# A two-block transformer kernel: attention sums that leave their result as columns, and transposes that also divide

## The reference, cut to what matters

```
# first block, each layer: six heads that share one k and one v
logits = q·k * 64 ** -0.5, -inf where the index or the causal mask says so
p = softmax(logits);  a_out = p @ v
mix = concatenate([a_out, b_out, c_out]) @ w_out[l];  x = x + g1 * mix

# second block, layer 0 (forgetting attention), 16 heads, each with its own v
s = q·k * scale + c_q - c_k;  o = softmax(s, causal) @ v;  h = h + o @ w_out

# second block, layer 1 (sparse attention), 16 heads, v shared by 8 heads
e_c = exp(s_c - max(s_c)) * m_c;  p_c = e_c / max(sum(e_c), 1.0)     # 15 compressed keys
o = g[0] * (p_c @ vc) + g[1] * (softmax(s_s) @ vs) + g[2] * (softmax(s_w) @ vw)
h = h + o @ w_out
```

## Time and profile before

| | |
|---|---|
| median of 3 runs | 2928.42 us (2925.82 to 2932.46) |
| the profiled execution | 2925.72 us, of it 2923.8 us span |
| PE busy | 2451.6 us, 84% of the span |
| DVE busy | 1976.5 us, 68% |
| ACT busy | 1412.9 us, 48% |
| attention of the first block, layer 0 | 178.4 to 198.3 us |
| the same, layer 1 | about 705 to 725 us |
| forgetting attention | 2081.7 to 2144.6 us |
| sparse attention | 2551.3 to 2687.6 us |

### The profile page before, as it was taken

The page is one execution under the profiler, slowest core; times in us unless marked ns, Lnnn a source line. Parts: engine busy times, 40 slices in busy tenths (PEclk is TensorE's granted clock), DMA queues, the critical chain, the costliest instruction groups (busy, mean ns, idle before and its releaser), DMA issues.

```text
span 2923.8 us, 31822 instructions
## 1 busy us (share of the span) xinstructions
PE 2451.6 (84%) x13007; PEld 2110.9 (72%) x13007; DVE 1976.5 (68%) x2434; ACT 1412.9 (48%) x1353; POOL 28.0 (1%) x52
## 2 busy tenths in 40 slices
PE   5847799883585999999999999959479975588898
PEld 4736699763464888888888888847479965567898
DVE  6555654756564888888888888865448864444787
ACT  5322444432332777777777777753334432344432
POOL 0000000000000000000000000000000000000000
PEclk9957899986686999999999999989689985666999
DMA  8501755741052999999999999974025541200453
GB/s 328 162 1 33 244 188 187 271 140 49 4 173 96 376 337 356 357 355 357 347 347 355 355 358 356 356 226 145 29 67 187 188 147 38 94 1 25 148 185 113
DMA packets 293723, 590.78 MB, mean 202 GB/s; under 512 B 11702, under 2 KB 86564, under 8 KB 292928
## 3 DMA queue, kind: packets, MB, share of 16 engines
q1 hardware_dynamic: 289872, 572.33, 55.5%
q0 software_dynamic: 3696, 16.32, 1.8%
HBM read 587.56 MB, written 1.05 MB: 201 GB/s over the span
## 4 chain that ended last, share of the span: by engine, by line
PE 60%; DVE 5%; ACT 2%; DMA 1%; issue 1%; POOL 0%; DVEq 0%; SPq 0%; ACTq 0%
PE ps L1084 17%; PE ps L1086 17%; PE ps L1085 17%; PE ps L1184 2%; PE ps L1167 1%; PE ps L1152 1%; PE ps L1282 1%; DVE arena L1589 1%; PE ps L1265 1%; PE ps L1243 1%; PE ps L1121 1%; PE ps L1138 1%; DVE arena L1732 0%; DVE Z L1598 0%; DVE Z L1589 0%
## 5 line engine op out<-in xcount | busy, mean ns | idle before, releaser
L764 ACT ACTIVATE w_hi<-raw 128x2048 fp32r<-128x2048 f32 x548 | 1041.9, 1906 | 635.1 <-PE ps L1086 505.0
L1574 DVE TENSOR_TENSOR w_lo<-raw,w_hi 128x2048 fp32r<-128x2048 f32 x548 | 1225.2, 2273 | 54.1 <-ACT w_hi L764 38.0
L1084 PE MATMUL ps<-w_hi,xT_hi 128*128 128x512 f32 (+3 forms) x1600 | 637.3, 398 | 43.0 <-DVE xT_lo L1678 24.3
L1086 PE MATMUL ps<-w_hi,xT_lo 128*128 128x512 f32 (+3 forms) x1600 | 623.4, 390 | 0.0
L1085 PE MATMUL ps<-w_lo,xT_hi 128*128 128x512 f32 (+3 forms) x1600 | 622.9, 389 | 0.0
L1084 PEld LDWEIGHTS ps<-w_hi,xT_hi 128*128 128x128 f32 x1600 | 306.5, 192 | 109.8 <-DVE xT_lo L1678 25.7
L1085 PEld LDWEIGHTS ps<-w_lo,xT_hi 128*128 128x128 f32 x1600 | 306.9, 192 | 62.3 <-issue 3.3
L1086 PEld LDWEIGHTS ps<-w_hi,xT_lo 128*128 128x128 f32 x1600 | 305.6, 191 | 62.2
L1084 PE MATMUL ps<-xT_hi,w_hi 128*128 128x256 f32 (+1 forms) x1120 | 324.6, 290 | 15.2 <-DVE xT_lo L2270 11.0
L1085 PE MATMUL ps<-xT_lo,w_hi 128*128 128x256 f32 (+1 forms) x1120 | 324.3, 290 | 0.0
L1086 PE MATMUL ps<-xT_hi,w_lo 128*128 128x256 f32 (+1 forms) x1120 | 324.1, 289 | 0.0
(11 more groups left out here) (315 smaller groups left out, 2052.8 us busy)
## 6 DMA issues: line engine op xcount, KB each, us to landing
raw<-in_moe_w_gate SPq DMA_DIRECT2D x112, 1024.0 KB, 5.4
raw<-in_moe_w_up SPq DMA_DIRECT2D x112, 1024.0 KB, 5.4
raw<-in_moe_w_down SPq DMA_DIRECT2D x112, 1024.0 KB, 5.5
raw<-in_w_ada SPq DMA_DIRECT2D x48, 1024.0 KB, 5.3
raw<-in_f_w_up SPq DMA_DIRECT2D x44, 1024.0 KB, 5.0
raw<-in_f_w_down SPq DMA_DIRECT2D x22, 1024.0 KB, 5.0
raw<-in_w_in SPq DMA_DIRECT2D x20, 1024.0 KB, 6.3
raw<-in_a_w_in SPq DMA_DIRECT2D x12, 1024.0 KB, 5.1
```

The costliest lines, as they stand in the source:

```text
L764: act.activation(w_hi[:, k % HI, 0:LEN[k]], raw[:, r, 0:LEN[k]], ACT.Copy).then_inc(w_hi_ready, 1)
L1084: pe.matmul(out_, lh, rh, start=start, stop=False)
L1086: return pe.matmul(out_, ll, rh, start=False, stop=stop)
L1574: dve.tensor_tensor(w_lo[:, k % RAW, 0:LEN[k]], raw[:, k % RAW, 0:LEN[k]], w_hi[:, k % HI, 0:LEN[k]].bitcast(F32), ALU.subtract).then_inc( ...
```

## The change

Three things change together, in all four attentions.

**The sums are turned.** The values become the stationary operand (64 columns) and the transposed probabilities the moving one. The result has features on the partitions: heads of even number on partitions 0 to 63, of odd number on 64 to 127, 128 tokens wide. Where heads share their values (first block, sparse attention) two heads of one parity go in one product of 256 columns. That is the column layout of the next linear: `out_high` (ScalarE) and `out_low` (VectorE) split the bank straight into `xT_hi` and `xT_lo`. The three parts of the sparse attention are now added in the bank by TensorE (`first`, `last`), one evacuation for three parts.

**The division moves.** Since tokens are now along the free dimension, the inverse row sum can't be multiplied on afterwards. `scaled(i)` on VectorE computes the inverses, multiplies with the gate, and writes a 128x512 tile of four diagonal matrices; the transposes of the probabilities become matmuls whose moving operand is that diagonal instead of the identity. They wait for `att_scaled`.

**`to_columns` goes.** Before `fa_out` and `nsa_out` it is removed; before `out0` and `out1` it starts at chunk 3 (ten tiles instead of sixteen).

```diff
@@ TensorE, transposed(i)
-                    if kind == "few":
-                        pe.wait_ge(att_probs, at.few(i))
-                    else:
-                        pe.wait_ge(att_exp, at.scored(i))
...
-                            last = pe.transpose(ps[0:kw, 6 + u // 4, (u % 4) * P:(u % 4 + 1) * P],
-                                                bufs[at.nth[i] % 3][:, x:x + kw], ident)
+                    pe.wait_ge(att_scaled, at.scored(i))
...
+                             last = pe.matmul(ps[0:kw, 6 + u // 4, (u % 4) * P:(u % 4 + 1) * P],
+                                              bufs[at.nth[i] % 3][:, x:x + kw],
+                                              diags[at.nth[i] % 2][:, h * P:(h + 1) * P], start=True, stop=True)
@@ TensorE, sums(i)
-                    for h in range(nh):
-                        for c in range(nch):
-                            u = h * nch + c
-                            last = pe.matmul(ps[:, 2 + s % 2, h * HD:(h + 1) * HD], Ts[s % 2][0:kw, u * P:(u + 1) * P],
-                                             v(h, c), start=c == 0, stop=c == nch - 1)
+                    n_v, shared = nh // 2, len(v) == 1
+                    for parity in range(2):
+                        out_ = ps[HD * parity:HD * parity + HD, 2 + o % 2, :]
+                        for j in range(1 if shared else n_v):
+                            w = n_v * P if shared else P
+                            for c in range(nch):
+                                x = ((c * 2 + parity) * n_v + j) * P
+                                last = pe.matmul(out_[:, j * P:j * P + w], v[0 if shared else 2 * j + parity](c),
+                                                 Ts[s % 2][0:kw, x:x + w], start=at.first[i] and c == 0,
+                                                 stop=at.last[i] and c == nch - 1)
@@ VectorE, in place of kept(i) and taken(i)
+                def scaled(i):
...
+                    dve.wait_ge(att_exp, at.scored(i))
+                    if kind == "few":
+                        x = bufs[s % 3][:, 0:nh * 256].rearrange("p (h w) -> p h w", h=nh)[:, :, 0:W]
+                        tt(x, x, kept.unsqueeze(1).to_broadcast([P, nh, W]), ALU.mult)
+                        step(dve.tensor_reduce(total, x, AX.X, ALU.add))
                     ts(total, total, 1.0, ALU.max)
                     step(dve.reciprocal(inverse, total))
+                    if weight is not None:
+                        tt(inverse, inverse, weight, ALU.mult)
...
+                    dve.tensor_tensor(diags[s % 2][:, 0:nh * P].rearrange("p (h t) -> p h t", h=nh),
+                                      ident.unsqueeze(1).to_broadcast([P, nh, P]),
+                                      inverse.unsqueeze(2).to_broadcast([P, nh, P]), ALU.mult).then_inc(att_scaled, 1)
...
+                for k in range(n + 4):
                     if k < n and at.parts[k][0] != "heads":
                         maxima(k)
-                    if 0 <= k - 3 < n and at.parts[k - 3][0] != "heads":
-                        taken(k - 3)
-                    if 0 <= k - 1 < n and at.parts[k - 1][0] == "few":
-                        kept(k - 1)
+                    if 0 <= k - 1 < n and at.parts[k - 1][0] != "heads":
+                        scaled(k - 1)
+                    if k >= 4 and at.last[k - 4]:
+                        out_low(k - 4)
@@ ScalarE, VectorE: the split into columns
+                    act.activation(hi, ps[:, 2 + o % 2, 0:at.parts[i][1] * HD].rearrange("p (k t) -> p k t", t=P),
+                                   ACT.Copy).then_inc(att_high, 1)
...
+                    dve.wait_ge(att_high, at.outs(i))
+                    dve.tensor_tensor(lo, ps[:, 2 + o % 2, 0:at.parts[i][1] * HD].rearrange("p (k t) -> p k t", t=P),
+                                      hi.bitcast(F32), ALU.subtract).then_inc(att_taken, 1)
@@ before the output linears
-                to_columns(mix)
+                to_columns(mix, 3)
                 linear(f"out{l}")
...
-            to_columns(mix)
             linear("fa_out")
...
-            to_columns(mix)
             linear("nsa_out")
```

More of the change, by code:

```diff
@@ L117, in __init__ @@
     def __init__(self, parts, count):
-        self.parts, self.nth, self._at = parts, [], []
+        self.parts, self.nth, self.first, self.last, self._at = [], [], [], [], []
         n = 0
-        for kind, _, _ in parts:
+        for kind, nh, W, turn in parts:
+            self.parts.append((kind, nh, W))
             self.nth.append(n)
+            self.first.append(turn in ("first", "only"))
+            self.last.append(turn in ("last", "only"))
             n += kind != "heads"
@@ L124, in __init__ @@
             count["scored"] += kind != "heads"
-            count["few"] += kind == "few"
+            count["outs"] += self.last[-1]
             self._at.append(dict(count))
@@ L132, in scored, with outs @@
         return self._at[i]["scored"]
-    def few(self, i):
-        return self._at[i]["few"]
+    def outs(self, i):
+        return self._at[i]["outs"]
     def scored_part(self, s):
@@ L490, in build @@
         att_T, fa_T, nsa_T = (attT, attT_b), (attT2, attT2b), (attT2, attT2c)
-        count = {"all": 0, "scored": 0, "few": 0}
-        dsa = [Attention([("full", nh, (b + 1) * P) for b in range(TB) for nh in (4, 2)], count) for _ in range(2)]
-        both = [("heads", 4, 66)] * 2
-        four = [("full", 4, (b + 1) * P) for b in range(TB)]
+        att_diag, late_diag = (diag_a, diag_b), (mix[:, 0, 0:512], mix[:, 0, 512:1024])
+        count = {"all": 0, "scored": 0, "outs": 0}
+        dsa = [Attention([("full", nh, (b + 1) * P, "only") for b in range(TB) for nh in (4, 2)], count) for _ in range(2)]
+        both = [("heads", 4, 66, None)] * 2
+        four = [("full", 4, (b + 1) * P, "only") for b in range(TB)]
         fa = Attention(both + both + four + both + four + both + four + four, count)
-        one = [("heads", 2, P)]
+        one = [("heads", 2, P, None)]
         def of_head(x, h):
@@ L503, in twice, with columns_of, dsa_places @@
             return x.unsqueeze(2).to_broadcast(shape)
-        six = [(kind, 4, W) for b in range(TB) for kind, W in (("few", N_CMP), ("full", (b + 1) * P), ("full", (b + 1) * P))]
+        six = [(kind, 4, W, turn) for b in range(TB) for kind, W, turn in
+               (("few", N_CMP, "first"), ("full", (b + 1) * P, None), ("full", (b + 1) * P, "last"))]
         nsa = Attention(one + one + six + one + six + one + six + six, count)
+        def columns_of(first, pairs, b):
+            return [x[:, first:first + pairs, b * P:(b + 1) * P] for x in (xT_hi, xT_lo)]
+        def dsa_places(i):
+            return columns_of(2 * (i % 2), 2 - i % 2, i // 2)
+        fa_places, nsa_places = (lambda i, at=at: columns_of(2 * ((at.outs(i) - at.outs(0) - 1) // TB), 2,
+                                                             (at.outs(i) - at.outs(0) - 1) % TB) for at in (fa, nsa))
         ar.at = a1
@@ L828, in experts, with to_columns @@
                 expert_rows(k)
-            def to_columns():
-                for k in range(4):
+            def to_columns(first=0):
+                for k in range(first // 2, 4):
+                    c = max(first, 2 * k)
                     act.wait_ge(tr_psum, got(tr_psum))
-                    act.activation(xT_hi[:, 2 * k:2 * k + 2, :],
-                                             ps[:, k, :].rearrange("p (k t) -> p k t", k=2), ACT.Copy).then_inc(xT_hi_ready, 1)
+                    act.activation(xT_hi[:, c:2 * k + 2, :],
+                                   ps[:, k, :].rearrange("p (k t) -> p k t", k=2)[:, c - 2 * k:2, :],
+                                   ACT.Copy).then_inc(xT_hi_ready, 1)
             def square_sums(src):
@@ L980, in _ @@
                 root(stat_b[:, 0:2])
-                to_columns()
+                to_columns(3)
                 linear(f"out{l}")
@@ L1113, in linear, with to_columns @@
                 got(lin_evac, min(2, gi))
-            def to_columns(src):
+            def to_columns(src, first=0):
                 pe.wait_ge(rows_ready, got(rows_ready))
-                for k in range(4):
-                    for c in (2 * k, 2 * k + 1):
+                for k in range(first // 2, 4):
+                    for c in range(max(first, 2 * k), 2 * k + 2):
                         for b in range(TB):
@@ L1739, in maxima @@
                                       ALU.mult).then_inc(att_centred, 1)
[L1741 to L1752 removed]
+                def scaled(i):
+                    kind, nh, W = at.parts[i]
+                    _, weight, kept = ops[i]
                     s = at.nth[i]
```

134 lines of the change are left out of this document (54 added, 80 removed).

## The result

The changed kernel takes 2955.05 us (median of 4 runs, 2951.05 to 2955.66), the kernel before 2930.44 in the runs beside it (4 runs, 2925.82 to 2933.10): a ratio of 1.0083, 95% interval 1.0070 to 1.0096. It is slower by 24.6 us; 17 were forecast. The profiled executions span 2952.9 and 2923.8 us, 29.1 apart: that of the kernel before took 2925.72 us, 4.7 under its median, that of the changed kernel 2954.88, its median, so the traces show a few us more than the medians do.

What follows compares the result with a forecast made beforehand. PE was taken as the bound, with gaps. Sparse attention +13 and -4.2, forgetting attention +8 and -5.1, first block +5.2 make +17 us on the median 2928.4: forecast 2945 us, range 2918 to 2980.

Steps and rivals of the forecast that it cites:

- The ring: In the attentions: scores, maxima of a part, diagonals and transposes of the part before, next scores; takes over 15.9 us of waits.
- part 2: Diagonals: `scaled` takes 1.35 us, 0.5 more on few parts; a sparse-attention group 39.9 us at half clock, 28.9 at full.
- rival (d): Diagonal products run in one pass; a sparse-attention group takes 33 or 25.5 us, about -13 in all, 2915 us; chance 5%.
- I take 45% of the time at full: PE's clock in the sparse attention: 45% of the time at full, so a group takes 34.1 us, the stage 149.
- rival (a): Wide products keep PE's clock at full; sparse attention 126 us, -28 in all, 2900 us; chance 15%, mostly 2900 to 2925.
- rival (b): PE's clock stays where it is or falls; all at half: sparse attention 174 us, +72, 3000; 15% for 2962 and more.
- The forgetting attention: Later first transposes and doubled passes over four groups, +8 us; its tail goes, -5.1 us.
- the second ones can start 0.6 to 0.9 us later: Forgetting attention: second transposes of a pair start 0.6 to 0.9 us later and take 16 passes instead of 8.
- The first block: Per layer 18 transposes become 36 passes and `scaled` is in the chain, +4 us; `to_columns` -1.4; two layers +5.2.
- The turned product costs what the old one did.: Turned sums, four heads, 128 keys at half clock: 1.76 us before, 1.71 after; one pass saved per part, 0.4 us.
- rival (c): Halves of the sums overlap fully: nothing in the sparse attention, -8 us in the forgetting one, 2937 us; chance 10%.
- PE the bound, with gaps: Kernel before, attention stages: PE busy 114.9 of 136.3 us in the sparse attention, 48.7 of 62.9 in the forgetting one.

Runs made afterwards that it cites:

- wait, one pass: Changed kernel with the diagonal step computed and waited for, but transposes by the identity in one pass, diagonals unused and division left out: 2927.05 us.
- experiment 2: Changed kernel with the sums of odd heads sent to the same 64 output partitions as even heads and added there: 2950.14 us.
- scores first: TensorE issues scores of part k ahead of the transposes of part k-2: changed kernel 2878.80 us, kernel before 2879.81 us.
- experiment 6: Kernel before, with the transposes of exponentials made matrix products by the identity, two passes instead of one: 2923.19 us, ratio 0.9973.
- experiment 1: Three kernels from the changed one: no diagonal step, one-pass transposes, 2869.01 us; the same, two passes, 2870.74; diagonals waited for but unused, one pass, 2927.05.

## Why the prediction was right, and where it wasn't

**The direction and the mechanism were right.** The ring that part 2 of the prediction set up is the one that the timeline shows, and it is what the transposes wait for: 43.4 us in 21 waits in the sparse attention. Both ways of cutting it (TensorE's order, VectorE's order) take time off, 76 and 40 us, of the 76 some 26 more than the same order takes off the kernel before. The diagonal tile takes 0.69 us as the earlier trace rows said (686 ns). Two passes per diagonal product, which rival (d) doubted, are there, at 0.23 us each at half clock (16 in 3.68) where 0.214 was taken. Of the signs that the prediction named, the sparse attention's clock (0.65, near 0.72 expected), its length (158, 145 to 155) and the forgetting attention's (74, near 71) were missed. All three stages were dearer than forecast.

**The ring's prices were right; the clock in it was not.** The prediction gave a group of the sparse attention 39.9 us at half clock and 28.9 at full, with 13 us around four groups. A granted clock of 0.65 means 30% of the time at full (0.5 + 0.5 x 0.30). Then a group takes 1 / (0.70 / 39.9 + 0.30 / 28.9) = 35.8 us, and the stage 4 x 35.8 + 13 = 156 us; 158.1 was measured. The same sum with the clock of other kernels that keep this ring:

| kernel | clock | the prediction's sum at that clock | measured |
|---|---|---|---|
| changed | 0.65 | 156 | 158.1 |
| sums on one half | 0.76 | 146 | 145.2 |
| products in the wait | 0.96 | 131 | 131.6 |
| wait, one pass (33 and 25.5 a group, from rival (d)) | 0.58 | 139 | 136.1 |

The step that failed is "I take 45% of the time at full": it was 30%. It makes 7 of the 9 us by which the sparse attention was mis-sized (158.1 against 149). The 45% were leaned on the forgetting attention's 0.74. Why the clock here stayed under it the runs don't show. The prediction named the ring's idle time under rival (a), as what speaks against the full clock, and didn't carry it into its own share; but idle time alone doesn't give the clock either: after the change PE is idle for 27% of the forgetting attention, at 0.74, and for 29% of the sparse one, at 0.65, and before the change it was idle for 17% of the sparse one, at 0.59. The table has the measured clock put in: it bears out the prediction's terms, not its forecast of the clock. One slip stands in rival (b): at half clock throughout its terms give 8 + 4 x 39.9 + 5 = 173 us, not 174.

**The forgetting attention** was forecast at +2.9 with its tail gone, and came to +6.8. The kernel with the wait and one pass has +1.0 at this point, so 5.8 are second passes, the upper end of what the prediction gave them (0.8 to 1.6 a group, so 3 to 6). Add the 5.1 of the tail to the 1.0, and the wait cost 6 us, where 0.6 to 0.9 a group, so 2.4 to 3.6, had been given. Here the step "the second ones can start 0.6 to 0.9 us later" was too small. All of this paragraph's differences are between single executions, good to 2 or 3 us.

**The first block** was forecast at +5.2 and came to +8.7 in its two layers. The reason given, that passes make the most of it, is not borne out: the kernel with the wait and one pass has +5.4 in the first layer, against +5.7, so there the wait makes most of it. In the second layer it has +1.8 against +3.0, too little to tell apart. With a few parts and no filling, `scaled` is bare in the chain; the prediction mentioned this and gave it no number.

**"The turned product costs what the old one did."** I priced a sum pass of 256 columns at 0.43 us at half clock with one pass in a part saved. It was 0.24: eight passes from 2607.03 to 2608.95 in the changed kernel, and 0.13 at full clock. The mechanism of rival (c) was real, and stronger than the central case had it. It brought nothing to see, as the prediction said of the sparse attention: the sums run while VectorE works. In the forgetting attention, where that rival put its 8 us, no run shows a gain either: with the overlap taken away (experiment 2) this stage was 1.6 us shorter, not longer, which is within what single executions differ by.

**Rival (a)** had about the right price for this stage and a condition that this change didn't meet: a full clock would make the sparse attention 126 us. With products in the wait it was 131.6 at 0.96, and the whole kernel 2923.5. This change alone leaves PE idle for 29% of the stage, and there the clock was 0.65.

**What the prediction missed altogether** is that it called PE the bound, with gaps, in the kernel before. It read 115 of 136 us busy. But the 115 us were no fixed amount of work: with scores first the same products take 97 us, at a clock of 0.70, and the stage 107. VectorE's 50.1 us in 24 waits for scores were to be read in the profile of before, and they pointed to a ring that was there already. "A ring that was not there" should have been "a tighter ring than the one there".

**On the two rules of the Trainium skill.** Perfetto Trace Analysis, section Transposes, prefers transposes to matmuls by the identity. In the kernel before, two-pass products by the identity were 0.27% faster than transposes (experiment 6); the measurement decides, and it goes against the rule as a rule of time for this kernel. Where the second pass stood behind the wait for the diagonals, though, it cost 28 us (experiment 1). TensorE: Matmul & The Clock Gate, Part 4, says that the full clock does not engage for transposes, as they don't count as busy in the same way. In the four pairs of kernels that differ in it the two-pass products had the higher clock in the sparse attention each time: 0.78 against 0.59, 0.65 against 0.58, 0.82 against 0.78, 0.87 against 0.78. Over the whole kernel too the clock is higher in every execution with two-pass products than in any of its partner's, in all four pairs. The last pair also differs in VectorE's step. The direction agrees; that it comes from the mode and not from the doubled work is not shown, since no run here has one without the other.

**What stays open.** Why the clock is 0.59 in the kernel before with PE busy for 83% of the stage, and 0.87 in the changed one with scores first with 84%. The two differ in the form of the sums, in the passes of the transposes and in the order, and no run takes these apart for the clock.

## What to carry to other kernels

Before pricing what a change adds to an engine, follow one part around all engines and ask which instruction stands between it and the next part on each; if that closes a ring, try the order first, since an exchange of two issue steps was worth 76 us here and 50 in the kernel before, three and two times what the change itself moved. A cost in such a ring can be paid (28 us for second passes behind the diagonals) where outside it it is hidden (2 us by the medians, if with a wide interval); and it can come back through the clock, as in the kernel before, where the same second passes made it 7 us faster. Only a run tells which.

And give TensorE's clock in the changed stage a range of its own in the sum, with a price at each end, instead of the value of another stage: the same ring took 158 us at 0.65 and 132 at 0.96, and neither the busy share nor the clock of before told which it would be.

## What the hardware showed that was not expected

Useless products in TensorE's idle time made the kernel 31 us faster (2955.1 to 2923.5): the granted clock in the sparse attention rose from 0.65 to 0.96. In the kernel before it went from 0.59 to 0.78 when each transpose became a product of two passes.

Products of 128 rows and 64 output columns that write different halves of the output partitions overlap, though one half's four passes come all before the other's: eight passes that stream 256 columns take 1.02 us at full clock, and 1.87 when all write the same half, in the same order.
